# Six buffers of split weights at six different offsets within 2048 bytes

## The reference, cut to what matters

```
for l in range(2):
    xn = rms_norm(x, norm_mix_g[l])
    xa, q, k, v, zc, xd = split(xn @ w_in[l])       # 1024 -> 2816 columns
    ya, yb, yc, yd = pool_mixer(xa), moba_attention(rope(q), rope(k), v), spatial_gating(gelu(zc)), conv_module(xd)
    gates = sigmoid(xn @ w_gate[l] + b_gate[l])     # 1024 -> 4 x 1024
    merged = sum of gates[i] * (y_i @ w_proj_i[l])
    x = x + merged @ w_o[l]
    hn = rms_norm(x, norm_ffn_g[l])
    g, u = halves of hn @ w_ffn_in[l]               # 1024 -> 2 x 2816
    x = x + (silu(g) * u) @ w_ffn_out[l]
return rms_norm(x, final_norm_g)
```

## Time and profile before

| what | value |
|---|---|
| median of 3 runs | 824.46 us (823.4 to 824.62) |
| span of the profiled execution | 823.8 us |
| TensorE busy | 814.7 us |
| VectorE busy | 615.2 us |
| ScalarE busy | 459.1 us |
| GpSimd busy | 149.6 us |
| read from HBM | 152.39 MB |

### The profile page before, as it was taken

One profiled execution on the slowest core, in us unless ns is written; L12 is line 12 of the kernel. 1 busy time (PEld: TensorE's weight loads), 2 busy tenths in 40 slices (PEclk: granted clock), 3 DMA queues, 4 the chain that ended last, 5 costly groups with the idle time before them and its releaser, 6 DMA issues.

```text
span 823.8 us, 12686 instructions
## 1 busy us (share of the span) xinstructions
PE 814.7 (99%) x4930; PEld 718.2 (87%) x4930; DVE 615.2 (75%) x741; ACT 459.1 (56%) x628; POOL 149.6 (18%) x145
## 2 busy tenths in 40 slices
PE   8999999999999999999999999999999999999997
PEld 8999887888989999999999988878899888888885
DVE  5899898877786667666787899988687667565664
ACT  6656687534564454444565577855355554445544
POOL 2407753083000000000000385513300000000000
PEclk9999999999999999999999999999999999999999
DMA  9985555567545564655568564555645465645451
GB/s 285 274 262 183 169 173 197 202 194 217 189 151 166 195 204 165 223 172 194 164 204 256 168 216 159 188 191 171 213 160 173 154 204 167 224 169 200 157 179 51
DMA packets 103740, 156.15 MB, mean 190 GB/s; under 512 B 4096, under 2 KB 69170, under 8 KB 103696
## 3 DMA queue, kind: packets, MB, share of 16 engines
q1 hardware_dynamic: 102224, 153.50, 56.3%
q0 software_dynamic: 1296, 1.79, 0.8%
q10 hardware_dynamic: 176, 0.27, 0.1%
HBM read 152.39 MB, written 1.05 MB: 186 GB/s over the span
## 4 chain that ended last, share of the span: by engine, by line
PE 96%; DMA 2%; DVE 1%; issue 1%; ACT 0%; SPq 0%; DVEq 0%; ACTq 0%
PE bank L1089 20%; PE bank L1091 10%; PE bank L1034 8%; PE bank L1036 8%; PE bank L1035 8%; PE bank L977 7%; PE bank L979 7%; PE bank L978 7%; PE bank L1066 5%; PE bank L1064 5%; PE bank L1065 5%; DMA raw<-in_w_in 1%; DMA gates<-in_x 1%; PE bank L1169 1%; PE bank L1190 1%
## 5 line engine op out<-in xcount | busy, mean ns | idle before, releaser
L1436 DVE TENSOR_TENSOR w_lo<-raw,w_hi 128x2048 fp32r<-128x2048 f32 x135 | 313.7, 2324 | 132.8 <-ACT w_hi L647 132.1
L647 ACT ACTIVATE w_hi<-raw 128x2048 fp32r<-128x2048 f32 (+3 forms) x146 | 264.2, 1816 | 129.6 <-PE bank L1036 56.6
L1089 PE MATMUL bank<-act,w_hi 128*128 128x512 f32 x704 | 247.8, 396 | 0.0
L1091 PE MATMUL bank<-act,w_lo 128*128 128x256 f32 x704 | 197.0, 280 | 0.0
L1089 PEld LDWEIGHTS bank<-act,w_hi 128*128 128x128 f32 x704 | 132.0, 188 | 30.3
L1091 PEld LDWEIGHTS bank<-act,w_lo 128*128 128x128 f32 x704 | 132.9, 189 | 0.4
L1034 PE MATMUL bank<-w_hi,act 128*128 128x512 f32 x288 | 114.4, 397 | 0.0
L1036 PE MATMUL bank<-w_hi,act 128*128 128x512 f32 x288 | 112.3, 390 | 0.0
L1035 PE MATMUL bank<-w_lo,act 128*128 128x512 f32 x288 | 112.1, 389 | 0.0
L647 ACT ACTIVATE qk<-bank 128x256 f32<-128x256 f32 (+1 forms) x96 | 37.5, 394 | 76.5 <-PE bank L1091 76.3
L977 PE MATMUL bank<-act,w_hi 128*128 128x256 f32 x256 | 73.1, 286 | 0.4 <-DVE w_lo L1779 0.4
(11 more groups left out here) (245 smaller groups left out, 1449.6 us busy)
## 6 DMA issues: line engine op xcount, KB each, us to landing
raw<-in_w_ffn_in SPq DMA_DIRECT2D x44, 1024.0 KB, 5.1
raw<-in_w_gate SPq DMA_DIRECT2D x32, 1024.0 KB, 5.5
raw<-in_w_ffn_out SPq DMA_DIRECT2D x22, 1024.0 KB, 4.9
raw<-in_w_in SPq DMA_DIRECT2D x18, 1024.0 KB, 6.0
raw<-in_w_o SPq DMA_DIRECT2D x8, 1024.0 KB, 5.1
raw<-in_w_proj_b SPq DMA_DIRECT2D x4, 1024.0 KB, 4.9
raw<-in_w_in SPq DMA_DIRECT2D x12, 256.0 KB, 6.9
gates<-qk SPq DMA_DIRECT2D x32, 64.0 KB, 4.8
```

The costliest lines, as they stand in the source:

```text
L647: return nc.scalar.activation(o, i, ACT.Copy)
L1089: nc.tensor.matmul(bank[b + f], hi[:, k, fs], act2[:, k, :, :].rearrange("p h s -> p (h s)"), start=(k == 0), stop=False, skip_group_check ...
L1091: last = nc.tensor.matmul(main(b)[:, f, :], lo[:, k, fs], act_hi[:, k, :], start=False, stop=(k == KT - 1), skip_group_check=True)
L1436: V.tensor_tensor(w_lo[slot][:, :], raw[slot][:, :], w_hi[slot][:, :].bitcast(F32), ALU.subtract)\
```

## The change

The lists of the buffers `w_hi` and `w_lo` are made in two loops that place small tensors, never read or written, between them. Against the place that each buffer had, the six now stand 0, 32 and 64 bytes (`w_hi` of slots 0, 1, 2) and 128, 256 and 512 bytes (`w_lo` of slots 0, 1, 2) later. A last pad of 512 bytes brings the sum to 1024, so that every tensor declared behind them starts 1024 bytes later than before. `raw` stays where it was. No instruction, wait, transfer or shape is changed.

```diff
         raw = [sb(f"raw{s}", [P, 8 * UC]) for s in range(RING)]
-        w_hi = [sb(f"w_hi{s}", [P, 8 * UC], F32R) for s in range(RING)]
-        w_lo = [sb(f"w_lo{s}", [P, 8 * UC], F32R) for s in range(RING)]
+        w_hi, w_lo = [], []
+        for s, gap in enumerate((0, 32, 32)):
+            if gap:
+                sb(f"gap_hi{s}", [P, gap // 4])
+            w_hi.append(sb(f"w_hi{s}", [P, 8 * UC], F32R))
+        for s, gap in enumerate((64, 128, 256)):
+            sb(f"gap_lo{s}", [P, gap // 4])
+            w_lo.append(sb(f"w_lo{s}", [P, 8 * UC], F32R))
+        sb("gap_x", [P, 128])
 
         x_res = sb("x_res", [P, KT, S])
```

## The result

The changed kernel takes 828.32 us in the median (827.69 to 829.16, 4 runs) against 824.21 us (823.40 to 824.62, 4 runs): a ratio of 1.0056, 95% interval 1.0044 to 1.0068. It is 4.1 us slower, where no change was forecast, and above the forecast range of 822.9 to 826.0 us.

What follows compares the result with a forecast made beforehand. TensorE was taken to bound the kernel; 823.8 us of span plus 0 each for VectorE, ScalarE and TensorE gave 823.8, and with the runs' median 0.66 us above the span, 824.4 us, range 822.9 to 826.0 us.

Steps and rivals of the forecast that it cites:

- What bounds the kernel: TensorE, busy 814.7 of 823.8 us, sets the end; only matmul pace or a split late enough to stall it matters.
- VectorE and ScalarE: Splits and copies: 0 on the path; bounds 8 ns more a split, 12 ns a copy; ten long splits beside GpSimd stay.
- TensorE: 4,930 matmuls keep their pace: 0 for the change, bounds +6.9 and -4.7 us.
- the first: TensorE: other engines don't disturb it; pairs take 0.347 us with and without splits beside them.
- The second: TensorE: within a unit weight blocks move by 1024 and 512 bytes, so operand distance modulo 2048 already changes all the time.
- The third argument: TensorE: same lines, tiles and slots run at 391 and 398 ns means, so the address does not choose the pace.
- The slower rival: Stages with 512 streaming columns: displaced weight buffers slow TensorE, up to 6.9 us, so 831.3 us; chance 0.09.
- The faster rival: FFN pairs and 256-column products: common remainder costs TensorE today, -4.7 us, so 819.7 us; chance 0.11.
- The smaller shift of pace: FFN units thrown into the other pace, ten of 44 worth 1 us: 823.4 or 825.4; counted half forecast, half rivals.
- Splits late: VectorE splits all 0.54 us slower: TensorE waits 0.42 us at 262.62 and 0.09 at 420.05, 824.9 us; chance 0.02.
- places not changed: The pads fail to move the buffers as the change says: time stays 824.4 us; chance 0.01.
- What the profile was to show: Unchanged durations if right; wrong if slots differ or line 1034 or 1065 on `y_hi` leaves 389 ns by over 2.

Runs made afterwards that it cites:

- The chains: Whole computation left out, TensorE alone runs 24 equal matmuls per chain at chosen operand offsets: 113.4 to 120.0 ns at 256 columns, 227 to 234.3 at 512.
- The chains after preludes: Computation left out, TensorE alone runs pairs or threes after 1 to 5 short matmuls: the pair at (64, 0) settled at 340 ns nine times, 353 six, 350 once.
- the kernel with starts by use and pairs at 0: Kernel before, each unit's split weights written at a start chosen by use, FFN pairs at 0 and 0: 820.33 us, ratio 0.9958.

## Why the prediction was wrong

**What bounds the kernel** was right. TensorE sets the end before and after, and the change of its steps, 4.4 us, is the change of the time.

**VectorE and ScalarE** were right: 0 on the path. The split has the same median of 2292 ns at six different distances, the copy is 3 ns slower, inside the bound of 12 given. The ten long splits stayed ten, all of them beside GpSimd instructions. (Another 24 of the 135 overlap a GpSimd instruction and are not long, before and after; what sets them apart was not looked for.) The rule of the Trainium skill that was weighed there (SBUF — State Buffer, Who interferes with whom), by which a VectorE instruction with two inputs in SBUF contends with a GpSimd instruction that reads SBUF, agrees with that: the addresses moved and the ten stayed, at up to 2827 ns against a median of 2292.

**TensorE** is the step that failed: "I take 0 for the change". Of its three arguments the first stands: a three of 512 columns takes 680 ns on TensorE alone, and the kernel before runs most of its threes on `act` and `y` at 680 too, with the splits beside them. The second was empty. I read that the weight block moves by 512 and 1024 bytes within a unit and that the pace doesn't change, and took it that distances don't matter. The chains show a period of 256 bytes, so all those distances were the same one, 0. The only other distance in the large stages was that of `ff`, 384 bytes, which is 128 modulo 256, and it did show another pace. I had the row, priced it at 5 ns, and set it aside. What the runs showed in place of the 0 is +4.4 us of steps: +5.5 in the 512-column stages on `act` and `y`, +0.9 on `ff`, -1.8 in the 256-column products on `act` and `y`, and -0.2 on the pairs. The third argument drew the wrong conclusion from a true row: two paces at the same addresses mean that the address is not the only thing, not that it is nothing. The chains after preludes show both at work: the distances bear on which steady paces exist, what runs ahead picks among them. The pairs before alternate between 347 and 353 ns from unit to unit in a like way.

**The slower rival** had the right cause and the right place. Its price of 1104 matmuls times 5 ns, 5.5 us, is what was measured, 4.18 + 1.34 = 5.5 us, but the match is luck. The rival took every matmul to go to the pace of `ff`, at distance 128, and modulo 256 only one half of each slot's weights was displaced, by 32, 64 or 128. Priced matmul by matmul from the single chains, that comes to 2.7 us; the same threes run alone come to 5.7. Two other terms were wrong. Its pairs were to lose 1.4 us and lost nothing (-0.19). And it had nothing at 256 columns, where the products on `act` and `y` won 1.8 us and those on `ff` lost 0.9. It had a chance of 0.09, since the evidence against it was of the two empty kinds above. It also named the price of one buffer displaced by 32 bytes as unknown; that offset is no special case, as 32 costs 5 ns at 512 columns in the chains, and 64, 96 and 128 cost 5 to 6.

**The faster rival** put the gain in the pairs and the 256-column products. The second half of it was real, and stands in the account with a minus; by starts chosen for each use it was had without the loss, in part (2.75 and 0.8 us on `act` and `y`). The pairs did not all go to a quicker pace: they moved both ways.

**The smaller shift of pace** was priced at up to 1 us. The experiments show more: with unchanged distances the pairs moved by +0.5 us in one kernel and by +2.6 us in another.

**Splits late** and **places not changed** did not occur.

**What the profile was to show** worked as a test: line 1065 on `y_hi` leaving 389 ns by more than 2 was named as the sign that the start address counts, and it went to 394. The other sign, slots that differ, came too (232.8, 231.6 and 233.2 ns).

## What to carry to other kernels

Where TensorE is the bound and float32 products with a new standing block for each matmul follow without a gap, the starts of the two operands are part of the tuning: look at their distance modulo 256 bytes for each stage, and measure chains in the kernel's own pattern of matmuls, as the best distance differs with the number of columns and the price of a pattern is not the sum of its matmuls. Before a row is used as evidence that some quantity doesn't matter, ask which values of it the row has in fact seen; here the steps within a unit were all multiples of 512. And a pace seen at unchanged addresses in two sizes is a sign of several steady states, so the effect of a placement on a whole kernel has to be measured, not added up.

## What the runs showed of the hardware

- The pace of a chain of matmuls in rounded float32, each with its own load, goes from 113.4 to 120.0 ns at 256 columns and from 227 to 234.3 ns at 512, by the distance of the two starts modulo 256 bytes. Steps below 32 bytes count too: +8 bytes gives 115.8 and 230.7 ns, +4 bytes 118.3 and 232.6.
- In a pattern of three the price is not the sum of the three: with only the low half of streaming weights displaced, by 128 bytes, the three took 693 ns in place of 680, where a single chain at that distance is 5 ns slower a matmul; with only the high half displaced by 64 bytes it took 702.
- The Trainium skill (TensorE: Matmul & The Clock Gate, Part 2, Step-by-step) gives TensorE two independent read ports and says that loading the next block takes no read bandwidth from the running matmul. The runs show that the time from one matmul to the next nevertheless depends on how the two starts lie to each other (227 or 234 ns at 512 columns). Through what part they meet, and whether it is a matmul's own two operands or the next load that counts, was not found.
- The same chain has several steady paces, 340 or 353 ns (once 350) for a pair at (64, 0), and keeps the one it fell into over the ten pairs measured; before, the pairs of the FFN ran at 347 or 353 ns.
- With unchanged distances modulo 256, step sums of a stage repeat from one kernel to another to 0.01 us in many cases (all eight kinds with offsets in multiples of 256), but not always: +0.14 us on the pairs with the rest moved by 1024 bytes, +2.6 us in the kernel with starts by use and pairs at 0.
- The copies of ScalarE and the subtractions of VectorE, with the buffers at six offsets from 0 to 512 bytes, keep their median and mean durations within 3 ns.
